# Moving a vector-matrix product from the pair stage into the pw2 stage, and sharing the context chunks of a two-directional recurrence

## What is computed

```
u = h @ w_in; cv, cg, cs, lx, ls = split(u)
v = silu(layernorm(conv(cv * sigmoid(cg))))
y_conv = (v @ pw2_w + pw2_b) * silu(cs)              # stage G2
x = x + (1 + gate) * (concat([y_conv, y_lru]) @ w_out)  # stage G3
sh1, sc1, g1, sh2, sc2, g2 = split(silu(c) @ ada_w + ada_b, 6)  # the last four are "late"
q, k, v, o, gates = split(h @ m_in_w + m_in_b)       # for 256 context and 1024 own tokens
# state of each direction: first over the 2 context chunks of 128, then over 8 own chunks
C_new = a * C + (ws * k)^T v
h = (w_inter * (q @ C) + s @ v) / max(|den|, exp(-m_t))
# the backward direction reads the same context chunks in the opposite order
```

## Time and profile before

| | us |
|---|---|
| median of 3 executions | 2099.24 (2098.36 to 2099.6) |
| the profiled execution | 2098.63 |
| its span (first to last instruction) | 2096.8 |
| PE busy | 2009.8 (96%) |
| DVE / ACT / POOL busy | 1308.7 / 845.4 / 1069.3 |
| PE clock, mean over the span | 0.979 of full |

### The profile page before, as it was taken

The page is one execution under the profiler, slowest core; times in us unless marked ns, Lnnn a source line. Parts: engine busy times, 40 slices in busy tenths (PEclk is TensorE's granted clock), DMA queues, the critical chain, the costliest instruction groups (busy, mean ns, idle before and its releaser), DMA issues.

```text
span 2096.8 us, 24126 instructions
## 1 busy us (share of the span) xinstructions
PE 2009.8 (96%) x9095; PEld 1658.2 (79%) x9095; DVE 1308.7 (62%) x1374; ACT 845.4 (40%) x1118; POOL 1069.3 (51%) x614
## 2 busy tenths in 40 slices
PE   6999999999999999989889999988999999999998
PEld 5788888888788888877677888766888888878877
DVE  6889998877741576865773565478655555523124
ACT  5343355556451313221334464445443344412134
POOL 1376755555212222332883446547878877722254
PEclk7999999999999998999999999998999999999999
DMA  9641121212113332533775875341222222253133
GB/s 377 211 146 38 51 76 54 73 56 63 43 59 101 105 107 71 185 100 126 256 249 155 286 261 145 107 151 60 61 61 59 72 91 81 71 190 123 46 88 126
DMA packets 269265, 250.38 MB, mean 119 GB/s; under 512 B 8330, under 2 KB 230291, under 8 KB 269155
## 3 DMA queue, kind: packets, MB, share of 16 engines
q1 hardware_dynamic: 253587, 231.08, 34.7%
q10 hardware_dynamic: 15568, 17.83, 2.4%
HBM read 205.03 MB, written 43.84 MB: 119 GB/s over the span
## 4 chain that ended last, share of the span: by engine, by line
PE 53%; issue 10%; POOL 6%; DVE 3%; DMA 1%; ACT 1%; SPq 0%; POOLq 0%; DVEq 0%; ACTq 0%
PE PS L2393 18%; PE PS L1882 12%; PE PS L2285 6%; PE PS L2146 5%; PE PS L2181 3%; POOL wl L905 2%; PE PS L2407 1%; PE PS L2229 1%; PE PS L2230 1%; PE PS L2238 1%; PE PS L1912 1%; POOL SCR L1038 1%; POOL wl L1024 1%; PE PS L2218 1%; PE PS L2071 1%
## 5 line engine op out<-in xcount | busy, mean ns | idle before, releaser
L905 POOL TENSOR_TENSOR wl<-raw,wh 128x1024 fp32r<-128x1024 f32 (+1 forms) x145 | 350.1, 2415 | 722.6 <-ACT wh L1184 506.6
L1882 PE MATMUL PS<-XH,wh 128*128 128x512 f32 x1232 | 382.1, 391 | 5.6 <-DVE XL L3233 1.7
L1882 PE MATMUL PS<-XH,wl 128*128 128x512 f32 x1232 | 380.8, 390 | 0.0
L1882 PE MATMUL PS<-XL,wh 128*128 128x512 f32 x1232 | 380.7, 390 | 0.0
L1882 PEld LDWEIGHTS PS<-XH,wh 128*128 128x128 f32 x1232 | 229.6, 188 | 55.6 <-issue 3.0
L1882 PEld LDWEIGHTS PS<-XL,wh 128*128 128x128 f32 x1232 | 230.4, 188 | 47.4
L1882 PEld LDWEIGHTS PS<-XH,wl 128*128 128x128 f32 x1232 | 230.2, 188 | 46.9
L1184 ACT ACTIVATE wh<-raw 128x1024 fp32r<-128x1024 f32 (+1 forms) x96 | 98.4, 1025 | 413.8 <-PE PS L1882 181.7
L2636 DVE SCALAR_TENSOR_TENSOR PS<-B,PJ,PS 128x1022 f32<-128x1022 f32 (+7 forms) x197 | 251.1, 1275 | 7.5
L1257 ACT ACTIVATE wh<-raw 128x1024 fp32r<-128x1024 f32 x48 | 50.9, 1060 | 245.8 <-PE PS L1882 228.5
L1115 POOL TENSOR_TENSOR wl<-SCR,wh 128x512 fp32r<-128x512 f32 x80 | 113.8, 1424 | 70.8 <-ACT wh L1710 70.8
(11 more groups left out here) (483 smaller groups left out, 4295.8 us busy)
## 6 DMA issues: line engine op xcount, KB each, us to landing
raw<-in_ffn_up_w SPq DMA_DIRECT2D x48, 512.0 KB, 4.0
raw<-in_w_in SPq DMA_DIRECT2D x40, 512.0 KB, 4.6
raw<-in_m_in_w SPq DMA_DIRECT2D x37, 512.0 KB, 4.0
SCR<-in_ada_w SPq DMA_DIRECT2D x32, 512.0 KB, 6.1
mod_tiles<-in_mod_w SPq DMA_DIRECT2D x16, 512.0 KB, 13.3
B<-in_ada_w SPq DMA_DIRECT2D x16, 512.0 KB, 4.6
raw<-in_w_out SPq DMA_DIRECT2D x16, 512.0 KB, 4.9
raw<-in_m_out_w SPq DMA_DIRECT2D x16, 512.0 KB, 4.1
```

The lines of the kernel that those rows point to most:

```text
L905: tt(wl[slot][:, 0:kc, :], raw[slot][:, 0:kc, :], wh[slot][:, 0:kc, :].bitcast(F32), ALU.subtract).then_inc(lo_done, 1)
L1882: last = mm(ps[:, c:c + step_n], W[:, k, :], Y[:, k, c:c + step_n], start=(seen == 0), stop=(seen == total - 1))
```

## The change

Eight edits, in the order of the program.

1. The 32 late tiles are loaded in G2, behind the weight units of tiles 2 to 7 in groups of 5, 5, 6, 6, 5, 5, through a ring of 5 buffers; each load but the first five waits until the sum that last used its buffer is done.
2. DVE adds them up between the evacuations of G2, into `ctx_mem`.
3. The 32 one-column products stand in the last G2 tile, two after each pair of matmuls from its seventh on; DVE finishes the late values after G2. POOL's two memsets at the end of G2 wait for the last late sum.
4. The transposes of the gate rows move from pair 4 to pair 2 and to another bank; the wait of pair 5 on `late_used` goes.
5. The weight sums of the first pair move from POOL to DVE, between `v_evac(2)` and `v_evac(3)`.
6. In the V stage `v_evac(1)` comes ahead of the eight `token_low`; ACT makes the high parts one unit later (units 9 to 12, 4, 4, 2, 2 of them).
7. The second context unit of a direction reads the k and v that the other direction loaded first, with a `U` of its own (two loads of 256 KB).
8. So slot 1 is free for the first output chunk (n = 2), which is loaded in pair 2 (direction 0) and in pair 5 (direction 1).

```diff
+            def late_load(n):
+                if n == 0:
+                    sp.wait_ge(*at("xl_G2", KD))
+                elif n >= 5:
+                    sp.wait_ge(*at("late_summed", n - 4))
+                h, k = divmod(n, KD)
+                sp.dma_start(late_t[n % 5], ada_w[P * k:P * (k + 1), D * (EARLY + h):D * (EARLY + h + 1)]).then_inc(ev(f"late_in{n % 5}"), 16)
+            for t in range(KD):
+                unit(G2.U + t, t % 2, cols_of(pw2_w, 0, KD, P * t))
+                for n in range(n_late, n_late + (LATE_AFTER[t - 2] if t >= 2 else 0)):
+                    late_load(n)
+                    n_late += 1
+                cs_load(t, t % 2, t // 2)
...
             pair_load(0)
-            sp.wait_ge(*at("tk_lo", 3 * HK))
-            for n in range(4):
-                late_load(n)
...
-                if s == 1:
+                if s == COLS_AT - 1:
...
-                if s < O_PAIRS - 2:
-                    for n in range(4 + 7 * s, 4 + 7 * (s + 1)):
-                        late_load(n)
-                elif s == O_PAIRS - 2:
-                    sp.wait_ge(*at("late_summed", LATE * KD))
+                elif s == 2:
                     for d in range(2):
                         chunk_load(0, d, 0, False)
-            sp.wait_ge(*at("late_ps", 1))
-            chunk_load(1, 0, 1, False)
+                    for o in range(2):
+                        sp.wait_ge(*at(f"proj_out{o}", 16 * (DIRECT[o] + K_PAIRS)))
+                    chunk_load(2, 0, 1)
             sp.wait_ge(*at("oq_used", 7 * (O_PAIRS - 1) + 4))
-            chunk_load(1, 1, 1, False)
...
+            for d in range(2):
+                sp.dma_start(CONTEXT_U[d], um_d[d, chunk_of(1, d), 0:HEADS]...).then_inc(ev(f"chunk_in{1 - d}0"), 16)
+            chunk_load(2, 1, 1)
+            for d in range(2):
+                chunk_load(3, d, slot_of(3))
...
-            pool.wait_ge(*at("xl_G2", KD))
+            pool.wait_ge(*at("late_summed", LATE * KD))
...
-                if 1 <= q <= 4:
-                    o_weight_sum(0, q - 1)
-                elif 6 <= q <= 9:
+                if 6 <= q <= 9:
                     o_weight_sum(1, q - 6)
...
-            HIGH_AT = {8: (0, 8), 9: (8, 9), 10: (9, 11), 11: (11, 12)}
+            HIGH_AT = {9: (0, 4), 10: (4, 8), 11: (8, 10), 12: (10, 12)}
...
+            def late_columns(step_n):
+                if step_n == 6:
+                    pe.wait_ge(*at("late_summed", LATE * KD))
+                for c in range(max(2 * step_n - 12, 0), min(2 * step_n - 10, LATE * KD)):
+                    ins = mm(LATE_PS[:, c:c + 1], late_acc[:, c * P:(c + 1) * P], ones[:], start=True, stop=True)
...
-                if q == 7 * (O_PAIRS - 1):
-                    pe.wait_ge(*at("late_used", 1))
+                if q == 7 * (COLS_AT + 1):
+                    pe.wait_ge(*at("cols_sb", 1))
...
+            for t in range(KD - 2):
+                g2_tile(t)
+                late_sums(sum(LATE_AFTER[:t]), sum(LATE_AFTER[:t + 1]))
...
+            v_evac(1)
             dve.wait_ge(*at("rows_out", 16 * 10))
             for m in range(2 * HK):
                 token_low(m)
...
-            v_evac(1)
...
             for k in range(HK):
                 t3_sum(k)
             v_evac(2)
-            late_sums(0, 4)
...
+            for n in range(4):
+                first_weight_sum(n)
             v_evac(3)
...
                     bank_sum_pair(s, n)
-                    if s < O_PAIRS - 2:
-                        late_sums(4 + 7 * s + n, 5 + 7 * s + n)
```

More of the change, by code:

```diff
@@ L447, in block_pair_kernel @@
         V_FIRST = 1 + Q_TILES
+        COLS_AT = 2
         PAIR_UNIT = Product.unit
@@ L546, in place_of, with slot_of, loaded, chunk @@
             return ORDER.index(j if d == 0 else NT - 1 - j)
+        def slot_of(n):
+            return 0 if n == 0 else (n + 1) % 2
+        def loaded(n):
+            return 64 * (n >= 0) + 48 * ((n - 1) // 2) if slot_of(n) == 0 else 48 * (n // 2)
+        CONTEXT_U = [ctx_mem[:, HQ * d:HQ * (d + 1)].rearrange("p (h t) -> p h t", h=HEADS) for d in range(2)]
+        def chunk(n, d):
+            if n == 1:
+                return M[1 - d]["slots"][0] | {"U": CONTEXT_U[d]}
+            return M[d]["slots"][slot_of(n)]
+        def landed_chunk(n, d):
+            if n <= 1:
+                return at(f"chunk_in{(d + n) % 2}0", 48 + 16 * n)
+            return at(f"chunk_in{d}{slot_of(n)}", loaded(n))
         def indices(k, slot, d):
@@ L639, in _ @@
             sp.wait_ge(*at("conv_ok", KD))
[L640 to L643, removed]
+            def late_load(n):
[5 more added lines that the diff above has]
+                sp.dma_start(late_t[n % 5], ada_w[P * k:P * (k + 1), D * (EARLY + h):D * (EARLY + h + 1)]).then_inc(ev(f"late_in{n % 5}"), 16)
+            n_late = 0
+            for t in range(KD):
[4 more added lines that the diff above has]
+                cs_load(t, t % 2, t // 2)
             for s in range(2):
@@ L736, in rows_store @@
                         sp.dma_start(dst, src).then_inc(ev("rows_out"), 16)
[L738 to L742, removed]
             def chunk_load(n, d, slot, outputs=True):
                 m = M[d]["slots"][slot]
-                if n >= 2:
+                if n == 3:
+                    for other in range(2):
+                        sp.wait_ge(*at(f"chunk_free{other}", 2))
+                elif n > 3:
                     sp.wait_ge(*at(f"chunk_free{d}", n - 1))
@@ L1053, in q2 @@
             def q2(j, d, slot):
-                m = M[d]["slots"][slot]
+                m = chunk(j + NC, d)
                 pool.wait_ge(*at("w_ok", 2 * j + (2 * NC + d + 1)))
@@ L1482, in context_weights @@
             def context_weights(n, d):
-                U = M[d]["slots"][n]["U"]
-                act.wait_ge(*at(f"chunk_in{d}{n}", 48))
+                U = chunk(n, d)["U"]
+                act.wait_ge(*landed_chunk(n, d))
                 f(U, U, ACT.Exp).then_inc(ev("w_ok"), 1)
@@ L2221, in heads @@
             def heads(k, slot, d, seq):
-                m, w = M[d]["slots"][slot], M[d]
                 n, x, j, y = indices(k, slot, d)
+                m, w = chunk(n, d), M[d]
                 final = is_final(x)
@@ L2990, in _ @@
                 token_low(m)
-            token_sum(2 * HK)
-            token_sum(2 * HK + 1)
-            v_evac(1)
-            token_low(2 * HK)
-            token_low(2 * HK + 1)
-            for m in range(2 * HK + 2, 3 * HK):
-                token_sum(m)
-                token_low(m)
+            for k in range(HK):
+                token_sum(2 * HK + k)
+                if k:
+                    token_low(2 * HK + k - 1)
+            token_low(3 * HK - 1)
             for k in range(HK):
@@ L3058, in update @@
                     C = M[d]["C"][:, h, :]
-                    stt(out=C, in0=C, scalar=M[d]["slots"][slot]["U"][:, h, last:last + 1], in1=DC[h % 2],
+                    stt(out=C, in0=C, scalar=chunk(n, d)["U"][:, h, last:last + 1], in1=DC[h % 2],
                         op0=ALU.mult, op1=ALU.add).then_inc(ev("c_ok"), 1)
```

115 lines of the change are left out of this document (55 added, 60 removed).

## The result

The kernel after takes 2077.95 us (median of 4; 2076.46 to 2078.64) beside 2098.8 for the kernel before in the same runs, a ratio of 0.9901 (95% interval 0.9884 to 0.9919): 20.9 us faster. In a second comparison the medians were 2075.95 and 2098.52, ratio 0.9893 (0.9878 to 0.9909), 22.6 us. The forecast was 2075.0 in a range of 2064 to 2085.

What follows compares the result with a forecast made beforehand. PE was taken as the bound, with POOL the bound in the pair stage beside the late sums. G2 +8.0, V stage 0, pair stage -28.2, recurrence -4.0 gave -24.2 from 2098.63: 2074.4, as median 2075.0; range 2064 to 2085.

Steps and rivals of the forecast that it cites:

- The account of 504 matmuls, columns, transposes, waits and half clock: Pair stage: matmuls 114.4, columns 7.2, transposes 0.7, waits 14.1, together 136.4 of 144.0 us; 4.6 more at half clock.
- The four parts of the gain: Pair stage: 7.2 columns, 14.1 waits, 4.6 half clock and 2.4 short gaps, given as a gain of 28.2 us.
- Foreseen +8.0: G2: columns cost 7.3 to 7.6 us, waits for sums and weights 0.5; bounds +7.3 and +15.
- the 9.6 I took: G2: POOL's low parts delay DVE's 32 late sums by 0.3 us each, 9.6 us, so DVE ends at 696.7.
- my upper bound, 14.3: G2: six POOL low parts of 2.39 us each block DVE for their whole length, 14.3 us; PE waits 4.1.
- The 5.1 us: Start of the recurrence: the first step with outputs comes 5.1 us earlier.
- the wait for chunk 3: Recurrence: chunk n = 3 lands 5.6 us after issue if alone; its use comes 0.5 to 1.9 us too early.
- a net of -4.0: Start of the recurrence: net change of -4.0 us, bounds -3.2 and -4.6.
- a net of -1.5: Start of the recurrence: net of -1.5 us if a chunk's two loads take 7.9 us, as with the queue full.
- The slower rival's chain: G2, 4%: DMA moves only 222 GB/s, a tile takes 18.9 us instead of 10.9, PE waits for `raw`: 2120 us.

## Why the prediction was right, and where it was off

**Pair stage.** Foreseen 115.7 us and a gain of 28.2; measured 115.0 and 28.7. The account of 504 matmuls, columns, transposes, waits and half clock closed to 0.7 us. The cause, POOL's operations stretched by DVE's sums, is shown by the two kernels that separate sums from loads; POOL's low parts in after take 1.31 to 1.32 us on average and wait for ACT. One reading was too strong: not each operation of POOL took 2.27 us beside the sums. By the earlier trace rows 50 of them took 89.9 us, 1.80 on average; in the trace about half are at 1.3 and half at 2.27. A pair then costs POOL 11 x 1.80 = 19.8 us, not 25.0, against 19.1 of PE: POOL was the bound by a little only, and that is in keeping with eight waits of 11.9 us in all. (The four parts of the gain add up to 28.3, not 28.2.)

**G2.** Foreseen +8.0. The columns cost 7.5 as worked out. The sums ended 0.7 us before PE wanted them: in the profile's own time 701.7, less the 4.9 us by which it began later, 696.8, where I had 696.7. That this agrees to 0.1 us is luck, for the path there was another. I spread the blocking as 0.3 us over each sum; in fact most sums were free (median 1285 ns) and six, one for each of POOL's six low parts, paid 1.1 to 2.2 us each, while POOL's operations took 2.39 to 2.40 throughout. All 32 took 51.0 us, 28 of them at 1.285 and 4 first ones at 0.75 would be 39.0; the 12.0 us of blocking lie midway between the 9.6 I took and my upper bound, 14.3, and DVE waited 2.5 us for loads on top. I had the loads at 377 GB/s, leaving out the slices of 290 to 334 that the earlier trace rows also has; they came at 349. That is 2.4 us more of blocking than I took and 2.5 of waiting. What made up for these 4.9 us: the first sum of a group of eight is a cheaper form, 0.75 us (2.1 less in all), only five evacuations stood between the first sum and the last, not six (1.3 less), and DVE left hardly a gap (0.6 us in all, where I had 0.05 behind each operation). The errors cancelled, and with 0 to 0.7 us of room it would have taken little for PE to wait.

Two of the six sums that were held up are first ones of a group, a `tensor_scalar` with one SBUF input:

```profile
641.20 2.56 DVE L2677 TENSOR_SCALAR ctx_memory<-SCR,CA 128x1024 f32<-128x1024 f32 x1 [0.24 <-DVE B L2811]
...
655.59 0.75 DVE L2677 TENSOR_SCALAR ctx_memory<-SCR,CA 128x1024 f32<-128x1024 f32 x1
...
671.25 2.89 DVE L2677 TENSOR_SCALAR ctx_memory<-SCR,CA 128x1024 f32<-128x1024 f32 x1 [0.65 <-DMA SCR<-in_ada_w]
```

Beside POOL's low parts they took 2.56 and 2.89 us, alone 0.75. The prediction gave the rule of the Trainium skill, page "SBUF — State Buffer", section "Who interferes with whom", too widely when it said that a DVE instruction with at most one SBUF input does not contend: the section excepts the 2-port modes, and names `tensor_scalar` among the instructions that can enter them.

Over all profiles the stretch from the opening to the V stage grew by 6.6 us (260.8 in four of before's kind, 267.4 in nine of after's), less than the columns alone; the scatter of that stretch, 3 us between executions, covers it.

**V stage.** Foreseen: the gain of edit 6 comes back as a wait for `v_evac(2)` of 6.5 us. It did, at 6.87, and undoing the edit changed nothing. What was foreseen too: the chain of t3 sums starting at 964 (977.2 in the profile, whose V stage began 12.4 us later: 964.8). The wait for a low part, which I had left at 3.0, became 3.4. DVE's timeline in after, the first of the t3 sums (line 2953) and `v_evac(2)` (line 2924):

```profile
977.21 0.68 DVE L2953 TENSOR_TENSOR B<-XH 128x512 f32<-128x512 f32 x1
...
987.47 1.88 DVE L2924 TENSOR_TENSOR B<-PS,SCR 128x512 f32<-128x512 f32 x3
```

The stage grew by 0.6 us in the first pair of profiles and by 2.1 in the second. These two waits together are 0.6 to 0.7 us longer than before, which covers the first; the rest of the second has no cause shown.

**Start of the recurrence.** The 5.1 us were right (5.1 in the first pair of profiles, 4.9 in the second). The term that was mis-sized is the wait for chunk 3: I took a load that lands alone in 5.6 us and a net of -4.0. In after the two directions' chunks are issued together, and `um_d` landed in 6.9 us, 1146.43 to 1153.3:

```profile
1146.43 0.62 SPq L784 DMA_DIRECT2D SCR<-um_d  x1
```

```profile
1153.31 0.66 PE L2229 MATMUL PS<-ident,SCR 128*128 128x128 f32 x4 [1.93 <-DMA SCR<-um_d]
```

The wait was 1.9 us, and the net -2.9 in one pair of profiles, -3.1 in the other, outside my bounds of -3.2 to -4.6. The landing lies between the 5.6 us that I took and the 7.9 us of a full queue, for which I had a net of -1.5; neither row fits alone.

**The sum.** 6.6 + 1.4 - 28.7 - 3.0 = -23.7 by the stages, -20.9 and -22.6 by the medians. I did not expect the opening and the stretch behind the recurrence to scatter by as much as they do. Over all profiles the opening lay 2.6 us later in after's kind and the stretch behind the recurrence was 1.4 us shorter; with these the sum is -22.5, beside the medians. What causes either is not shown, and the forecast of 2075.0 against 2077.95 and 2075.95 is as near as this scatter allows to say. The slower rival's chain is shown at twice the late traffic, and the change stayed clear of it: PE had no wait for weights in G2.

**Why there was anything to gain.** In both places the late sums run beside PE's matmuls. In the pair stage, however, PE depends on POOL in 11 operations every 19 us, and in G2 in one every 10.9. The sums cost PE 16 us in the one; in the other they delay DVE by 12 us, and PE, which needs them only in the last tile, hardly at all.

## What to carry to other kernels

Look not only at whether an engine has time for a piece of work, but at whom the work disturbs: here DVE was free enough in the pair stage, and its sums stretched about half of POOL's operations from 1.29 to 2.27 us, just where POOL fed PE. Before moving an operation ahead in an engine's queue to end a wait, read what then stands in front of the next one of its kind; the wait came back at the next pass, and moving both gave the 9 us. Where single executions scatter by several us, compare stages, not totals.

## What the runs showed that I had not expected

- The blocking between DVE and POOL came nearly whole: POOL ahead by 0.05 us, DVE's sum 3.42 instead of 1.285, POOL's 2.39 untouched. In the pair stage, where both ran back to back, each side paid (POOL a mean of 1.80 for 1.29, DVE a median of 1.58 for 1.285).
- With twice the late loads the 16 DMA engines moved 400 to 423 GB/s in 22 of 33 slices of 2.75 us, and no slice shows more. G2 of after used 349 on average over 65 us.
- The same program, after, began G2 at 618.5 us in one execution and at 623.1 in another.
